# Two trunk layers of a diffusion backbone: from one pass over all tokens per layer to two shifted streams

## The reference, cut to what matters

```python
sh1, sc1, gt1, sh2, sc2, gt2 = modulation(cvec, w_mod, b_mod)   # context: c_ctx, latent: c
h = rmsnorm(x, g_norm1) * (1 + sc1) + sh1
zin = h @ w_in                          # split: attention | SSD (xbc, dt, z) | conv (GLU)
o_attn = mla_attention(...) @ w_attn_out          # 16 heads
y_ssd = ssd_bidirectional(...)                    # chunks of 128 tokens, two directions
o_ssd = rmsnorm(y_ssd * silu(z), g_ssd_norm) @ w_ssd_out
o_conv = conformer_conv(...)                      # depthwise conv of 31 taps, layernorm, w_cv_pw2
gates = sigmoid(h @ w_gate + b_gate)
x = x + gt1 * ((g_a * o_attn + g_s * o_ssd + g_c * o_conv) @ w_out)
h2 = rmsnorm(x, g_norm2) * (1 + sc2) + sh2
x = x + gt2 * peer(h2)

def peer(h):      # per token: 8 heads, 16 of 128 x 128 experts each = 128 experts
    s = einsum(h @ w_q, keys); top 16 of each half, top 16 of the 256 sums -> e, g = softmax
    act = gelu(u[e] . h) * g            # u, v: (16384, 1024) per layer
    return sum(act * v[e])
```

## Time and profile before

| | |
|---|---|
| median of 3 runs | 3836.2 us (3834.5 to 3839.2) |
| the profiled execution | 3826.2 us, span 3824.4 us |
| busy: PE, PEld, DVE, ACT, POOL | 2769.3, 1366.1, 2117.8, 728.1, 982.4 us |
| moved by DMA | 1001 MB, of it gathers 805 MB |
| mean granted TensorE clock | 0.851 of 2.4 GHz |

### The profile page before, as it was taken

The page is one execution under the profiler, slowest core; times in us unless marked ns, Lnnn a source line. Parts: engine busy times, 40 slices in busy tenths (PEclk is TensorE's granted clock), DMA queues, the critical chain, the costliest instruction groups (busy, mean ns, idle before and its releaser), DMA issues. The chain is left out here.

```text
span 3824.4 us, 41999 instructions
## 1 busy us (share of the span) xinstructions
PE 2769.3 (72%) x15738; PEld 1366.1 (36%) x15738; DVE 2117.8 (55%) x5029; ACT 728.1 (19%) x1614; POOL 982.4 (26%) x868
## 2 busy tenths in 40 slices
PE   6999999997656544544479998999976565455453
PEld 3556755565111101111045567555751111011010
DVE  1316797126685677555413168971367756765554
ACT  1114311112222111111111142211122221111111
POOL 0000310002444444444300004000025444444442
PEclk9999899999888767766689998999988887677776
DMA  5221322233999999999852313314249999999997
GB/s 206 106 104 67 114 97 88 113 120 154 421 405 383 421 421 385 422 421 421 365 204 88 126 45 133 121 45 154 79 203 421 383 404 421 410 407 421 421 421 330
DMA packets 130764, 1001.17 MB, mean 262 GB/s; under 512 B 14960, under 2 KB 16304, under 8 KB 21500
## 3 DMA queue, kind: packets, MB, share of 16 engines
q0 software_dynamic: 110592, 805.36, 51.0%
...
...
## 5 line engine op out<-in xcount | busy, mean ns | idle before, releaser
L1862 PE MATMUL bank<-arena 128*32 128x512 f32 x3072 | 579.4, 893 | 908.3 <-DVE arena L2021 908.3
L2012 DVE CUSTOM_DVE_ANT_0 arena<-arena 128x1024 f32<-128x1024 f32 x768 | 926.9, 1225 | 514.6 <-DMA arena<-in_experts_dram,arena 502.4
L1742 POOL DMA_INDIRECT arena<-in_experts_dram,arena x768 | 877.0, 1142 | 1245.0 <-PE bank L1862 887.9
L1862 PEld LDWEIGHTS bank<-arena 128*32 128x32 f32 x3072 | 102.9, 141 | 1327.5 <-DVE arena L2021 1082.9
L1780 ACT COPY arena<-bank 128x512 f32<-128x512 f32 x512 | 300.3, 587 | 451.0 <-PE bank L1845 439.1
L745 DVE SCALAR_TENSOR_TENSOR arena<-arena,vec 128x399 f32<-128x399 f32 (+1 forms) x576 | 322.3, 634 | 0.0
L795 PE MATMUL bank<-hT,arena 128*128 128x384 f32 x896 | 289.3, 486 | 0.0
L1562 PE MATMUL bank<-hT,arena 128*128 128x384 f32 x768 | 259.0, 491 | 0.0
L1786 ACT ACTIVATE arena<-arena 128x4 f32<-128x4 f32 x192 | 39.6, 206 | 1143.2 <-DVE arena L2012 1143.2
L1562 PE MATMUL bank<-arena 128*128 128x384 f32 x768 | 255.5, 486 | 0.0
L1845 PE MATMUL bank<-hn,consts 128*32 128x512 f32 x2048 | 244.4, 632 | 0.0
...
## 6 DMA issues: line engine op xcount, KB each, us to landing
arena<-in_w_big_dram SPq DMA_DIRECT2D x80, 2048.0 KB, 8.2
arena<-in_experts_dram,arena POOLq DMA_INDIRECT x768, 12.6
...
```

Of the source, the lines that this page charges most:

```text
L1742: nc.gpsimd.indirect_dma_start(row(k), None, io["experts"], bass.IndirectOffsetOnAxis(ap=ei[:, t % 2, n:n + 1], axis=0))\
L1862: mm = nc.tensor.matmul(K.ps[ACC[c]][32 * a:32 * a + 32, :], Z[:, j % 2, a, 28 - 4 * r:60 - 4 * r], rw[:, D + c * 512:D + (c + 1) * 512], ...
L2012: nc.vector.tensor_tensor_reduce(out=U_rows, in0=U_rows, in1=spread_h[:, n_use % NH, :], scale=1.0, scalar=0.0, op0=ALU.mult, op1=ALU.add, ...
```

## The change

The four parts "context, layer l" and "latent, layer l" of the front become objects of a class `Front`, and the experts of each become an object of a class `Experts`. There are five phases, each one block of programs with a barrier behind it:

| phase | front | beside it, experts of | ring places |
|---|---|---|---|
| 0 | context, layer 0 | none | 3 |
| 1 | latent, layer 0 | context, layer 0 | 3 |
| 2 | context, layer 1 | latent, layer 0 | 2 |
| 3 | latent, layer 1 | context, layer 1 | 3 |
| 4 | none | latent, layer 1 | 3 |

In a phase both streams are lists of labelled steps. `merged_order` lays them into one list: the experts' steps are spread evenly over the front's weights, to end at a given fraction of them (0.95 in phases 1 and 3, 1.06 in phase 2). Every engine runs its part of both streams in the order of that list (`run`), weight loads and spread loads on SP too. The 31-tap convolution is cut into 62 pieces of four taps and laid between all steps from the latents' or context's `cqT` to the gates of the second branch. Bands of the front's matmuls now have 128 or 256 token columns, and every weight block but the 12 of the modulation is loaded once for each part.

The context's experts (`split`) gather u and v rows separately, 4 KB each, into four places each, and load the spread tokens by DMA from a copy of h2 in memory. The latents' experts gather whole rows into 8 places (12 in phase 4) and spread by matmuls as before. `XG`/`XW` issue the gathers of a batch, `XS` the spread, `XD` the dots, `XZ` Gelu and Z, `XV` the matmuls on v, `XF` (every eighth batch) folds the result into x. Routing of a front's first tile is one step, `route`, at its end; the second latent tile is routed in pieces (`XR`) between the batches. The front has six PSUM banks where experts run beside it, and eight in phase 0. Fewer, wider instructions write the permuted indices. The front's own computation is otherwise that of before, per part.

The diff, cut to its core:

```diff
-def experts(K, l):
...
-            for step, t, i in expert_order():
...
+def ssd_order(F):
+    units = F.units
+    for i in range(len(units) + 1):
+        if i < len(units):
+            yield "AB0", units[i]
+            yield "AB1", units[i]
+        if i >= 1:
+            u = units[i - 1]
+            yield "YD", u
+            if not F.context:
+                yield "YO", u
+            if F.state_of(u):
+                yield "CS", u
+        if i < len(units):
+            yield "MX", units[i]
...
+def front_order(F):
+
+    steps = list(front_steps(F))
+    labels = [s[0] for s in steps]
+    pieces = -(-CW * KD // CONV_PIECE)
+    first, last = labels.index(("cqT", 0)), labels.index(("bra", 1, 0, 3))
+    done = 0
+    for i, (label, groups) in enumerate(steps):
+        if first <= i < last:
+            while done < pieces * (i - first + 1) / (last - first):
+                yield ("conv", done), []
+                done += 1
+        yield label, groups
+        if F.context and label in LATE_AT:
+            m = LATE_AT[label]
+            yield ("mod", m), [(("mod", m), "act", ("big", W_MOD + m))]
...
+class Experts:
+
+
+
+    def __init__(self, l, front, split):
+        self.l, self.tiles, self.n, self.c = l, front.tiles, front.n, front.c
+        self.h2, self.ei, self.gpm = front.h2, front.ei, front.gpm
+        self.split = split
+        self.batches = NQ * self.n
+        if split:
+            self.spread, self.g2, self.fl = 14080, 17152, 18176
+            self.U, self.V = [19200 + D * i for i in range(4)], [23296 + D * i for i in range(4)]
+            self.ahead = 1
+        else:
+            self.spread, self.g2, self.fl = 23692, 26764, 27788
+            self.s2, self.small = front.off["s2"], front.off["small"]
+            self.rows = [28812 + 2 * D * i for i in range(6)] + [8192, 10240]
+            if l == DEPTH - 1:
+                self.rows += [0, 2048, 4096, 6144]
+            self.ahead = len(self.rows) // BATCH

+NH = 3
+ROUTE_PIECES = 19
+def experts_order(X):
+
+    nb = X.batches
+    for b in range(X.ahead):
+        yield ("XG", b), []
+        if X.split:
+            yield ("XW", b), []
+
+    def spread(b):
+        return ("XS", b), [] if X.split else [(("XS", b, c), "xact", None) for c in range(2)]
+
+    for b in range(NH):
+        yield spread(b)
+    for b in range(nb):
+        yield ("XD", b), []
+        if b + NH < nb:
+            yield spread(b + NH)
+        if X.split and b + 1 < nb:
+            yield ("XG", b + 1), []
+        if not X.split and X.n > 1:
+            if b < ROUTE_PIECES:
+                yield ("XR", b), []
+            if b == ROUTE_PIECES:
+                yield ("XR", b), []
+                yield ("XP", 0), [(("XP", 0), "xdve", None)]
+        yield ("XZ", b), []
+        yield ("XV", b), []
+        if X.split and b + 1 < nb:
+            yield ("XW", b + 1), []
+        if not X.split and b + X.ahead < nb:
+            yield ("XG", b + X.ahead), []
+        if b % 8 == 7:
+            yield ("XF", b // 8), [(("XF", b // 8, c), "xdve", None) for c in range(2)]

+def weight(label):
+
+    return {"glu": 7.0, "bra": 7.2, "out": 5.2, "pq": 3.6, "q": 1.9, "cqkv": 5.0, "xbc": 3.6, "z": 5.0, "mod": 4.0, "conv": 0.5,
+            "route": 50.0, "yz": 3.0, "oT": 0.7, "yT": 0.7, "n1": 1.2, "n2": 1.2, "K": 1.5, "QT": 1.0, "SS": 1.5, "PT": 1.5,
+            "PV": 1.5, "AB0": 2.5, "AB1": 2.5, "YD": 2.5, "YO": 1.5, "CS": 1.5, "h2": 3.0}.get(label[0], 1.0)
+
+
+def merged_order(front, experts, end):
+
+
+    a, b = list(front), list(experts)
+    if not a or not b:
+        return a + b
+    total = sum(weight(s[0]) for s in a)
+    out, at, j = [], 0.0, 0
+    for s in a:
+        at += weight(s[0])
+        while j < len(b) and (j + 1) / len(b) * end <= at / total:
+            out.append(b[j])
+            j += 1
+        out.append(s)
+    return out + b[j:]

+class Phase:
+
+
+    def __init__(self, front, experts, ring, end=1.0):
+        self.F, self.X, self.ring = front, experts, ring
+        steps = merged_order(front_order(front) if front else [], experts_order(experts) if experts else [], end)
+        self.order = [s[0] for s in steps]
+        self.G = Groups(range(6) if experts else range(BANKS))
+        self.chunks, self.last, self.last_label = [], {}, {}
...
+        self.place, self.before, self.holds = {}, {}, {}
+        for n, chunk in enumerate(self.chunks):
+            s = n if n < ring else min(self.holds, key=lambda j: self.order.index(self.last_label[self.holds[j]]))
+            self.place[chunk], self.before[chunk] = s, self.holds.get(s)
+            self.holds[s] = chunk

+def run(order, *programs):
+
+    heads = [next(p, None) for p in programs]
+    for label in order:
+        for i, p in enumerate(programs):
+            while heads[i] == label:
+                heads[i] = next(p, None)
+    assert all(h is None for h in heads), heads
...
+def weights_sp(K, sp, p):
+
+    ph = K.phases[p]
+    at = 0
+
+    def after(chunk):
+
+        nonlocal at
+        i = ph.order.index(ph.last_label[chunk])
+        if i > at:
+            at = i
+            yield ph.order[i]
+
+    if ph.F is not None:
+        for n in range(K.prefetched, min(ph.ring, len(ph.chunks))):
+            K.load_chunk(sp, ph, n)
+        for n in range(ph.ring, len(ph.chunks)):
+            old = ph.before[ph.chunks[n]]
+            yield from after(old)
+            K.wait_full(sp, ph.last[old])
+            K.load_chunk(sp, ph, n)
+    K.prefetched = 0
+    if ph.F is not None and p + 1 < len(K.phases) and K.phases[p + 1].F is not None:
+        nxt = K.phases[p + 1]
+        places = sorted((ph.order.index(ph.last_label[ph.holds[s]]), s) for s in range(min(ph.ring, nxt.ring)))
+        for _, s in places:
+            yield from after(ph.holds[s])
+            K.wait_full(sp, ph.last[ph.holds[s]])
+            K.load_chunk(sp, nxt, s)
+        K.prefetched = len(places)
...
@@ in front_dve
+        if step == "conv":
+            yield label
+            if label[1] == 0:
+                K.wait_taken(dve, ("a", KD - 1))
+            for _ in range(CONV_PIECE):
+                next(pieces, None)
...
+        if step == "route":
+            yield label
+            K.wait_taken(dve, ("ps", 0, 3))
+            dve.wait_ge(S["h2_ready"], n)
+            for _ in route_dve(K, dve, steps, off["s"], off["small"], F.l * NKEYS * NKEYS, S["soft_in"]):
+                pass
+            gates_dve(K, dve, steps, off["small"], S["soft_exp"], S["perm_in"])
...
@@ in front_pe
+        if step == "pq":
+            yield label
+            m = label[1]
+            if m == 0:
+                K.wait_taken(pe, ("n2", n - 1, 1))
+            by_features(label, ("big", W_PQ + m // 4), m % 4, hT)
...
@@ experts_pool
+    for label in K.ph.order:
+        step = label[0]
+        if step not in ("XG", "XW"):
+            continue
+        yield label
+        b = label[1]
+        if b == NQ:
+            pool.wait_ge(S["xpermuted"], 1)
+        for q in range(BATCH):
+            col = (b // NQ) * SLOTS + BATCH * (b % NQ) + q
+            if X.split:
+                if b and step == "XG":
+                    pool.wait_ge(S["dot_done"], BATCH * (b - 1) + q + 1)
+                if b and step == "XW":
+                    pool.wait_ge(S["v_done"], b)
+                place, src, k = (X.U[q], half_rows, q) if step == "XG" else (X.V[q], half_rows, 4 + q)
+                dst = K.at(place, D)
+                if step == "XW":
+                    col += SLOTS
+            else:
+                k = (BATCH * b + q) % R
+                if BATCH * b + q >= R:
+                    pool.wait_ge(S["v_done"], (BATCH * b + q - R) // BATCH + 1)
+                dst, src = K.at(X.rows[k], 2 * D), io["experts"]
+            nc.gpsimd.indirect_dma_start(dst, None, src, bass.IndirectOffsetOnAxis(ap=ei[:, col:col + 1], axis=0)).then_inc(K.landed[k], 16)
...
@@ experts_sp
+    for label in K.ph.order:
+        if label[0] == "XS" and X.split:
+            yield label
+            b = label[1]
+            if b >= NH:
+                sp.wait_ge(S["dot_done"], BATCH * (b - NH + 1))
+            src = bass.AP(tensor=K.h2_rows.tensor, offset=4 * b * D, ap=[[D, 4], [0, 32], [1, D]])
+            sp.dma_start(spread[:, b % NH, :], src).then_inc(S[f"spread_landed{b % NH}"], 16)
...
@@ experts_act
+        if step == "XS" and not X.split:
+            yield label
+            if b >= NH:
+                act.wait_ge(S["dot_done"], BATCH * (b - NH + 1))
+            for c in range(2):
+                name = ("XS", b, c)
+                K.wait_full(act, name)
+                K.took(nc.scalar.copy(spread[:, b % NH, c * 512:(c + 1) * 512], K.bank(name)[:, :]), name)
+        if step == "XZ":
+            yield label
+            act.wait_ge(S["dot_done"], BATCH * (b + 1))
+            if b >= 2:
+                act.wait_ge(S["z_ready"], b - 1)
```

(70 more changed lines are left out.)

3190 lines of the change are left out of this document (1559 added, 1631 removed).

## The result

The change takes 4339.9 us (median, 4338.3 to 4347.6) against 3836.1 before: 13.2% slower, ratio 1.132 [1.130, 1.134]. The forecast was 3898 with a range to 4130; the direction was right (slower had 0.53), the size was not. The profiled execution has a span of 4339.6 us.

The account below looks back on a forecast made before the run. TensorE was taken to bound the front (VectorE its SSD loop) and row gathers the experts; phases of 515 + 873 + 953 + 873 + 652, plus 14 and 8, gave 3888 us, 3898 on the median, range 3670 to 4130.

Parts of the forecast that it names:

- The price of the cut fronts: Fronts cut into context and latent parts: 515 us for layer 0's context front alone, 768 for the latent front alone.
- The hole at the routes: At each front's end, 60 us with only routing on VectorE; in phase 2 a DMA hole, +42 us.
- DMA is the bound: Phase 2: 356 MB at 421 GB/s take 846 us, above TensorE's 535 and VectorE's 645; 953 with added terms.
- 45 for ring and attention: Phase 2: two block slots in place of three, and stages where VectorE comes last, together +45 us.
- both are in phase 2's 45: Phase 2: XV's wait for Z with front groups behind it, and spreads holding 2 of 6 banks, counted within 45 us.
- Beside the bound, at nothing: ScalarE's table loads, 328 us in all and 164 in phase 2, were to cost no time there.
- 4% for handovers: Phases 1 and 3, attention and SSD: VectorE-bound, 125 and 107 us become 131 and 111 with 4% added.
- the 25 us of waits in the branches: Phases 1 and 3, branches: 25 us of waits, including blocks late behind spread loads, within 216 us.
- rival 1: All five phases overlap as their larger engine allows, near the lower bounds: 3691 us on the median, chance 0.27.
- rival 2: TensorE's clock falls to 0.85 in TensorE-bound stages of the phases with two streams: 4078 us, chance 0.17.
- rival 3: The streams do not overlap, lookahead is used up at every step, engines wait for the slower stream: 4530 us, chance 0.04.
- The rule on the queues: Phases 1 and 3: DMA engines alternate queues by packet, blocks beside gathers move at half rate; 80 us more, 3978.

Follow-up runs that it names:

- e4: The change with XZ (Gelu and Z) moved right behind XD in the order, XV left in place: 4193 us median, phase 2 1081.
- e5: The change with XZ behind XD, spread loads later, conv pieces outside attention and SSD, route cut in 20, experts of phases 1 and 3 to the end: 4044 us.
- e14: The change with five order repairs combined and XV one batch later in all expert phases, so one batch of lookahead in phase 2: 4283 us, phase 2 1228.

## Why the prediction was right and wrong

**Right.** The price of the cut fronts: 742 us for the latent one against 768, 518 for the context one against 515; phase 4 668 against 652. In phase 1 attention (133 against 131), z (35, as reckoned), and output with the PEER queries (116 against 110) were within 6 us. SP's spread loads and ScalarE's tables cost nothing in phases 1 and 3, as reckoned. The hole at the routes is there: 77 and 106 us. Attention's hit is in part luck: alone it took 81 us where I had 95, so the experts added 52 and not 36. And that the change would be slower stood at 0.53, little better than a coin.

**Wrong: phase 2, 217 of the 442 us.** The step that failed is "DMA is the bound", 846 us plus small terms. DMA was busy 0.77 and the phase took 1061 us with a quarter of the rows' bytes. I had added each engine's work and taken the largest; with the lookahead of two batches each of the 64 batches is a chain (rows land, dots, Gelu, Z, v matmuls, places free, gathers asked), and the front's steps stand in the middle of it on both engines. Moving XZ up in the order, ahead of the routing piece and whatever front steps lay between, gave 88 us; one batch less of lookahead cost 186. The conv pieces gave 27, the cut route 10, the ring of two 32 (with quarter rows; it is 86 alone), leaving out the Gelu's tables 37. These are not parts of the 217 that can be summed: my 953 already held 42 for the route and 45 for ring and attention, and tables and Z lie on the same chain. What the runs do say: Z, conv pieces and route together brought phase 2 to 1040, and 87 over the forecast remain. The wait on Z was in the sum only as "both are in phase 2's 45"; TensorE waited 277 us for it there. "Beside the bound, at nothing" was wrong for the tables in phase 2.

Two terms of the sum were too small besides. DMA itself is busy some 900 us and not 846: 0.77 x 1169 in the change, 0.83 x 1081 in e4, 0.86 x 1040 in e5 and 0.73 x 1228 in e14 all give 894 to 900. The bytes were right (359 MB against 356), but beside other work they do not move at the plateau's 421 GB/s; which may be some 50 of the 87 us that remain in e5 (an estimate from these shares, for the part of the phase that DMA bounds). TensorE had 693 us to do and not 535: v matmuls and spreads 327 against 230, the rest in the front.

**Wrong: phases 1 and 3, 104 and 121 us.** The step is "4% for handovers", and the 25 us of waits in the branches. By stage the miss of phase 1 is in the branches (262 against 216), SSD (133 against 111), the route (77 against 66), the stages ahead of attention (140 against 130) and those between attention and SSD (81 against 74). Each amount that the experts add counts about a third to three quarters (dots 36 of 101, v 21 of 27), where I let it count only on the engine that was the bound. The wait for Z, which my sum named in phase 2 only, adds 26 us by the moved label alone, and 47 with nearly empty experts and late v matmuls. In the route, 12 us are the last fold, for which VectorE waits. No run gave the context's experts a second batch of lookahead or whole rows, so what that choice costs beside the latent front is not known.

**The rivals.** Full overlap (rival 1) failed by everything above. The clock (rival 2): in the branches of phase 1 it was granted 0.90, as feared, but 0.94 in the same stretch of the latent front alone. TensorE was busy 705 us in phase 1 where I had 625 (566 for the front, 59 for v). The front alone already takes 600, so 34 of these 80 us were a mistake of mine about the front; the v matmuls take 78, 19 over; and the front's own part is 628 beside the experts, 28 more than alone. That last is the clock's share, an upper end of it, so it is a consequence and small. No overlap (rival 3, 4530) was nearest in number, but its premise is wrong: phase 1 took 978 us and its two streams end to end 1335, as the split experts alone cost 593.

The rule on the queues of the Trainium skill, "DMA: Bandwidth & Descriptors", section "Queues, rings and completion order", had given 80 us to contention in phases 1 and 3 together. Quarter rows moved those phases by 31 and 51 us, 82 together, by all that shorter rows change. So the runs allow it as a term of that size, no more; that the turns of the queues are the reason no run shows.
